# A two-block transformer kernel: ring order carried through, output squares summed one stage earlier, the start of each product stage rearranged

## The reference, cut to what matters

```python
def pre(t, mm, i, gi):            # adaptive norm ahead of a projection
    return rms_norm(t, g[gi]) * (1 + mm[:, :, i + 1]) + mm[:, :, i]
def post(t, y, mm, i, gi, wres):  # norm of the projection's output, then the residual
    return t + wres * mm[:, :, i + 2] * rms_norm(y, g[gi])
# first block, DEPTH = 2 layers
h  = post(h,  swiglu(pre(h,  m,  0, 0), ffn_wi[0], ffn_wo[0]), m,  0, 1, 0.5)
hc = post(hc, swiglu(pre(hc, mc, 0, 0), ffn_wi[0], ffn_wo[0]), mc, 0, 1, 0.5)
...   # attention mixers between w_in and w_o, on h (and hc unless last)
h  = post(h, o @ w_o, m, 3, 3, 1.0)
h  = post(h, swiglu(pre(h, m, 6, 4), ffn_wi[1], ffn_wo[1]), m, 6, 5, 0.5)
...   # the same for hc, unless last

# second block, DEPTH = 2 layers: SSD + mLSTM mixer, then gated linear attention
for i in range(DEPTH):
    h = _rmsnorm(x, norm_g[i, 0])
    h = mixer(h)          # ends in concatenate([y, hm], -1) @ w_out, or o @ w_out
    x = x + _rmsnorm(h, norm_g[i, 1])
    f = _conv_ffn(_rmsnorm(x, norm_g[i, 2]), ...)   # gelu(gate) * val after a 3-tap conv
    x = x + _rmsnorm(f, norm_g[i, 3])
# rms_norm(x, g) = x * rsqrt(mean(x * x) + eps) * g; the output is x
```

## Time and profile before

| | |
|---|---|
| median of 3 timed runs | 2901.91 us |
| the profiled execution | 2906.06 us |
| its span, first to last instruction | 2904.3 us |
| TensorE busy with matmuls | 2690.8 us, 93% |
| VectorE, ScalarE busy | 1311.2 us (45%), 1174.9 us (40%) |
| DMA moved | 375.50 MB, mean 129 GB/s |
| mean granted TensorE clock | 0.954 |

### The profile page before, as it was taken

How to read it: one execution, slowest core, us unless ns; L and a number is a source line. 1 busy time by engine, 2 the same in 40 slices (tenths; PEclk the granted TensorE clock), 3 DMA queues, 4 the chain that set the end, 5 groups by cost and what they waited for, 6 DMA issues and landing times. The chain is left out here.

```text
span 2904.3 us, 39475 instructions
## 1 busy us (share of the span) xinstructions
PE 2690.8 (93%) x16552; PEld 2294.4 (79%) x16552; DVE 1311.2 (45%) x1671; ACT 1174.9 (40%) x1622; POOL 42.4 (1%) x80
## 2 busy tenths in 40 slices
PE   5999998998999998999998989989977899898998
PEld 3677786876677785888786879979966899897998
DVE  3222235455322234322336654455555576555675
ACT  3222225444322225332235544444355465353653
POOL 2000000000000002000000000000000000000000
PEclk8999999999999998999999989989987999898999
DMA  8666422212566524232231225435400354341443
GB/s 277 212 208 217 152 73 87 59 59 80 174 206 204 170 102 99 82 103 87 87 102 59 88 92 191 179 124 183 149 1 30 125 191 166 116 146 59 156 166 114
DMA packets 277162, 375.50 MB, mean 129 GB/s; under 512 B 11020, under 2 KB 232696, under 8 KB 276896
## 3 DMA queue, kind: packets, MB, share of 16 engines
q1 hardware_dynamic: 228240, 300.50, 31.1%
q10 hardware_dynamic: 46576, 69.26, 7.1%
q0 software_dynamic: 2208, 3.73, 0.9%
HBM read 372.33 MB, written 1.16 MB: 129 GB/s over the span
## 5 line engine op out<-in xcount | busy, mean ns | idle before, releaser
L464 PE MATMUL ps<-uh,wh 128*128 128x256 f32 (+1 forms) x4160 | 1396.8, 336 | 54.2 <-DVE ul L834 30.8
L465 PE MATMUL ps<-ul,wh 128*128 128x256 f32 (+1 forms) x4160 | 1381.2, 332 | 0.0
L466 PE MATMUL ps<-uh,wl 128*128 128x256 f32 (+1 forms) x4160 | 1379.3, 332 | 0.0
L464 PEld LDWEIGHTS ps<-uh,wh 128*128 128x128 f32 x4160 | 800.2, 192 | 170.5 <-issue 70.0
L455 DVE TENSOR_TENSOR wl<-ring,wh 128x2048 fp32r<-128x2048 f32 x212 | 482.1, 2275 | 889.2 <-ACT wh L450 784.3
L466 PEld LDWEIGHTS ps<-uh,wl 128*128 128x128 f32 x4160 | 800.4, 192 | 73.2
L465 PEld LDWEIGHTS ps<-ul,wh 128*128 128x128 f32 x4160 | 800.7, 192 | 69.7 <-issue 0.7
L450 ACT ACTIVATE wh<-ring 128x2048 fp32r<-128x2048 f32 x156 | 298.4, 1914 | 714.3 <-PE ps L466 349.8
L1066 DVE TENSOR_TENSOR wl<-ring,wh 128x2048 fp32r<-128x2048 f32 x66 | 151.3, 2293 | 324.0 <-ACT uh L1084 286.1
L1063 ACT ACTIVATE wh<-ring 128x2048 fp32r<-128x2048 f32 x66 | 126.3, 1914 | 340.1 <-PE ps L466 320.7
L1493 ACT ACTIVATE wh<-ring 128x2048 fp32r<-128x2048 f32 (+2 forms) x38 | 70.0, 1842 | 122.4 <-PE ps L466 122.2
(11 more groups left out here) (315 smaller groups left out, 2033.6 us busy)
## 6 DMA issues: line engine op xcount, KB each, us to landing
ring<-in_ffn_wi_dram SPq DMA_DIRECT2D x88, 1024.0 KB, 7.5
arena<-in_w_ada_dram ACTq DMA_DIRECT2D x42, 1536.0 KB, 6.7
ring<-in_ffn_w_up_dram SPq DMA_DIRECT2D x44, 1024.0 KB, 7.2
ring<-in_ffn_wo_dram SPq DMA_DIRECT2D x20, 2048.0 KB, 7.8
ring<-in_ab_w_in_dram SPq DMA_DIRECT2D x13, 2048.0 KB, 7.8
ring<-in_ffn_w_down_dram SPq DMA_DIRECT2D x10, 2048.0 KB, 7.8
ring<-in_c_w_in_dram SPq DMA_DIRECT2D x6, 2048.0 KB, 8.0
ring<-in_w_in_dram SPq DMA_DIRECT2D x20, 512.0 KB, 6.0
```

What stands on the lines that cost most here:

```text
L464: pe.matmul(to, sh, mh, start=start and n == 0, stop=False)
L465: pe.matmul(to, sh, ml, start=False, stop=False)
L466: mm = pe.matmul(to, sl, mh, start=False, stop=stop and last)
```

## The change

Seven edits, all of them of order and place; the arithmetic of the result is the same but for the order of one sum and of the accumulation in `ab_out`.

1. **Ring order.** `first` is no more given by hand. Each matrix begins in the slot after the last tile of the one before, so its tile 0 goes into the slot that is freed first, and tile 1 into the other.
2. **Output squares.** `Residual.tensor` becomes `tail_tensor`, in the producing stage, after its last product: TensorE multiplies the sum of the first seven squares and then the last square by ones, both into one bank. VectorE adds one square fewer.
3. **`high_of(1)`** stands ahead of the squares of `h` where T = 256.
4. **Fill.** Chunks of the second granule stand between those of the first: chunk 0 after chunk 4 for T = 512; chunks 0, 1, 2 after chunks 2, 4, 6 for T = 256.
5. **Down.** For T = 256 the split of the down projection's first input goes into the unused half of `uh` and `ul`, with no wait for the up products, and the second granule's split of the down weights is moved behind the last gate.
6. **`ab_out`.** The SSD half of the inputs is made in VectorE's loop of the `mlstm` stage, and the products of granules 0 and 1 stand between the transposes.
7. **End.** The stage `residual` is merged into `finish`: transposes follow each update of `h`, ScalarE copies eight times 128 x 256, and four stores of 256 KB take the place of two of 512 KB.

```diff
         def planned(key, weights):
+            if order:
+                before = plan[order[-1]]
+                weights.first = (before.first + before.n) % RING
             plan[key] = weights
...
                     load(sp, w, (turn + 1) * RING + k, k)       # before
+                    load(sp, w, (turn + 1) * RING + k, w.slot(k))
...
                     self.post.scalar(act)
+                    if self.n_s == 1:
+                        high_of(1)
                     for k in range(KD):
 
                         act.wait_ge(h_updated.sem, h_updated.at(k + 1))
                         act.activation(self.sq[:, k, :], h[:, k, 0:T], ACT.Square).then_inc(h_squared.sem, 1)
-                        if k == 2:
+                        if k == 2 and self.n_s == 2:
                             high_of(1)
...
-                    if k == 0:
+                    if k in (0, KD - 1):
                         continue
                     dve.wait_ge(y_squared.sem, y_squared.at(k + 1))
...
-            def tensor(self, pe):
-                pe.matmul(self.sum_bank(), ones, self.acc, start=True, stop=True).then_inc(y_summed.sem, 1)
+            def tail_tensor(self, pe):
+                pe.wait_ge(y_added.sem, y_added.at(KD - 2))
+                pe.matmul(self.sum_bank(), ones, self.acc, start=True, stop=False)
+                pe.wait_ge(y_squared.sem, y_squared.at(KD))
+                pe.matmul(self.sum_bank(), ones, self.ysq[:, (KD - 1) % 2, :], start=False, stop=True).then_inc(y_summed.sem, 1)
...
+            return [] if norm.post is None else [4] if norm.n_s == 2 else [2, 4, 6]
...
                 for kk in range(KD):
                     norm.input_ready(pe, kk)
+                    last = chunk(0, kk)
+                    if kk in beside:
+                        chunk(1, beside.index(kk))
                 last.then_inc(prod.sem, 1)
+                for kk in range(len(beside), KD):
+                    last = chunk(1, kk)
+                last.then_inc(prod.sem, 1)
...
-                            if g == KF - 1:
-                                down.input_high(act, 0)
-                            down.high_ahead(act, g - (KF - 2))
+                        elif g == KF - 2:
+                            down.high_ahead(act, 0)
+                        else:
+                            down.input_high(act, 0)
...
+                    def scan_chunk(k):      # in the mlstm stage, once for each head
+                        dve.scalar_tensor_tensor(out=scan_made[:, k // 2, k % 2, :], in0=mixed[:, k, :], scalar=col("ssd_norm", k),
+                                                 in1=group_rstd[:, k // 4, :], op0=ALU.mult, op1=ALU.mult)
...
+                    turned(0)
+                    for q in range(half - 1):
+                        for i in range(2):
+                            pe.wait_ge(u_ready.sem, u_ready.at(2 * q + i + 1))
+                            for g in range(AHEAD):
+                                products(g, (KD * i + 2 * q, KD * i + 2 * q + 1), q == 0 and i == 0, False)
+                            if i == 0:
+                                turned(q + 1)
```

More of the change, by code:

```diff
@@ L315, in two_blocks, with __init__ @@
         class Weights:
-            def __init__(self, n, loads, parts=1, count=None, split=True, looped=True, first=0):
-                self.first = first
+            def __init__(self, n, loads, parts=1, count=None, split=True, looped=True):
+                self.first = 0
                 self.n, self.loads, self.parts, self.split = n, loads, parts, split
@@ L480, in tile_loaded @@
             if w.looped:
-                pe.wait_ge(ready[k].sem, ready[k].at((turn + 1) * 16 * w.parts))
+                pe.wait_ge(ready[w.slot(k)].sem, ready[w.slot(k)].at((turn + 1) * 16 * w.parts))
             else:
@@ L1222, in granule @@
                     ada.rows(pe, g)
-            first()
+            first_two()
             if ada is None:
-                turns(pe, KF, 4, granule, 1)
+                turns(pe, KF, 4, granule, 2)
             else:
-                for g in range(1, KF):
+                for g in range(2, KF):
                     granule(g // 4, g % 4)
@@ L1239, in ffn1 @@
             key = ("up", l, f)
-            down = Down(key, ("down", l, f), mid, T, tail, ada)
+            down = Down(key, ("down", l, f), mid, T, tail, dve_free, ada)
             pairs = 4 if ada is None else 2
@@ L1273, in granule @@
                         act.activation(gates[:, k, 0:T], ps[:, 2 * (k % pairs), 0:T], ACT.Silu).then_inc(gate_done.sem, 1)
+                        if not more and g == KF - 1:
+                            down.high_ahead(act, 1)
                     if ada is not None:
@@ L1294, in granule @@
                                           ALU.mult).then_inc(dve_free.sem, 1)
+                        if not more and g == KF - 1:
+                            down.low_ahead(dve, 1)
                     norm.vector(dve, lambda g: low_of(0, g))
@@ L1348, in tensor @@
                                         [((vh[:, kk, c], vl[:, kk, c]), (self.xh[:, kk, 0:self.T], self.xl[:, kk, 0:self.T]))
-                                         for kk in self.order], before=self.input_ready if g == 0 and m == 0 else None)
+                                         for kk in range(self.n_k)], before=self.input_ready if g == 0 and m == 0 else None)
                         if g == self.n - 1 and m < self.G - 1:
@@ L2050, in latent, with finish, _ @@
                 s_.passed(KD)
-        def finish():
-            tokens = Arena().take(ST, D)
+        def finish(r):
+            tokens = Arena(KD * T2).take(ST, D)
+            halves = [slice(0, D // 2), slice(D // 2, D)]
             with stage() as block:
+                @block.scalar
+                def _(act):
+                    if r is not None:
+                        r.scalar(act)
+                    for k in range(KD):
+                        act.wait_ge(pe_step.sem, pe_step.at(k + 1))
+                        act.activation(tokens[:, :, k * P:(k + 1) * P], ps[:, k, S:T2].rearrange("p (t c) -> p t c", t=ST),
+                                       ACT.Copy).then_inc(act_step.sem, 1)
@@ L2076, in _ @@
-                    sp.wait_ge(stored.sem, stored.at(16 * ST))
+                    for i, c in enumerate(halves):
+                        sp.wait_ge(act_step.sem, act_step.at((i + 1) * KD // 2))
+                        for t in range(ST):
+                            sp.dma_start(out[0, t * P:(t + 1) * P, c], tokens[:, t, c]).then_inc(stored.sem, 16)
+                    sp.wait_ge(stored.sem, stored.at(16 * 2 * ST))
         CF = Arena()
@@ L2085, in ffn2 @@
             key = ("up2", i)
-            down = Down(key, ("down2", i), mid2, S, tail)
+            down = Down(key, ("down2", i), mid2, S, tail, conv_done)
             n_ch = 2 * KF
@@ L2830, in ab_out @@
             AHEAD = 2
-            mem = Arena(ROWS_END + 2 * 2 * S + 12 * ML_HEADS + 2 * S)
-            made = mem.take(4, 2, S)
-            assert mem.at <= ARENA
+            made = Arena(HN_AT).take(2, 2, S)
             half = KD // 2
-            pairs = [p_ for q in range(half) for p_ in ((0, q), (1, q))]
             place_of = lambda i, q: slice(KD * i + 2 * q, KD * i + 2 * q + 2)
+            source = lambda i, q: made[:, q % 2] if i else scan_made[:, q]
             with stage() as block:
@@ L2858, in _, with turned @@
                 def _(pe):
-                    for q in range(half):
+                    def turned(q):
                         pe.wait_ge(act_step.sem, act_step.at(q + 1))
@@ L2864, in _, with products @@
                         tr.then_inc(pe_step.sem, 1)
-                    w.tensor(pe)
+                    def products(g, ks, start, stop):
+                        _, shaped = w.granule(g)
+                        vh, vl = shaped(wh[side(w.key, g)]), shaped(wl[side(w.key, g)])
+                        return multiply(pe, ps[:, g, 0:S], [((vh[:, kk, :], vl[:, kk, :]), (w.xh[:, kk, :], w.xl[:, kk, :])) for kk in ks],
+                                        start=start, stop=stop)
+                    turned(0)
@@ L2898, in ab_out @@
             w.done()
-        AB_ORDER = [k for q in range(KD // 2) for i in range(2) for k in (KD * i + 2 * q, KD * i + 2 * q + 1)]
         GM = Arena()
```

220 lines of the change are left out of this document (118 added, 102 removed).

## The result

The changed kernel takes 0.9853 times the time of the kernel before, with a 95% interval of 0.9828 to 0.9879. In microseconds its three runs are 2854.03, 2859.69 and 2864.61, against 2901.23 (median of four): 41.5 us less. (A fourth execution took 5613.93 us, nearly twice the others; no trace shows why, and it stands in no comparison.) In a later comparison the same kernel gave 2862.83 us and 0.9857 (0.9840 to 0.9873). The forecast was 2869 us, 2858 to 2883: 33 us of gain, about 42 measured (41.5 and 42.1 in the two comparisons).

What follows compares the result with a forecast made beforehand. TensorE, busy 2690.8 of 2904.3 us, was taken to bound the kernel, leaving 213.5 us idle to gain from. Terms of -14.3, -5, +1.9, -6.85, -5.5, -3.4 summed to -33.2 us: median 2901.9 to about 2869, range 2858 to 2883.

Steps and rivals of the forecast that it cites:

- edits 1 and 2, product to Ln: Ten boundaries, last product to Ln: falls to 3.1 us (T = 512) or 1.5 (T = 256); -14.3 us, ends -7 and -17.
- edit 3, Ln to product, T = 256: Five boundaries: splitting granule 1 before the squares of h saves between 2.75 and 12.5 us; -5 taken.
- edit 4, fill: First granules: -0.9 for T = 512, +2.8 at four T = 256 boundaries; sum +1.9 us, ends -2 and +5.
- edit 5, up to down: Waits of 1.45 us go at three places, 2.16 at two, a new one near 1 comes; -6.85 us, ends -2 and -9.
- edit 6, ab_out: Products begin near 2229.5 instead of 2240.72, granule 2 then waits for its split; -5.5 us, ends -1.5 and -7.
- edit 7, the end: Program end: barrier goes, most transposes and copies run beside the updates; -3.4 us, ends -1 and -4.
- the ring order gates nothing: Tile late in its new slot too, at the boundaries; first two edits worth 1 us, not 14.3; 2882 us, chance 0.07.
- the one that makes `ab_out` worth nothing: Clock stays at 0.51 through ab_out's 96 matmuls: no gain there, fills cost 5 us; 2877 us, chance 0.15.
- at the low clock only the 0.63 goes, -0.55: Sums of h, T = 256: TensorE is slower than ScalarE at the low clock, so each boundary gains just its idle time.
- up to 0.75 us late: T = 256 boundaries: five chunks of granule 1, 3.6 us, cover granule 2's split, so granule 2 starts late by this.
- The figure that I had named from the Trainium skill: Final stores: a transfer takes some 2.0 us plus bytes over 436 GB/s; half-size store saves another 0.6 us, left unsummed.
- the third rival: Shorter TensorE stops at boundaries put sums of h at clock 1.00: another -7.5 us, 2861 us, chance 0.12.

Runs made afterwards that it cites:

- the first experiment: Changed kernel with the ring order undone, each matrix's first slot again given by hand: 2877.57 us, 0.9915.
- the better version: Changed kernel without fill at T = 256, output squares summed in producing stage only there, ab_out's granule 1 held back, lead behind squares at two boundaries: 2847.79 us, 0.9808.

## Why the prediction was right, and where it was not

The time lay in the range, 6 to 10 us below the likeliest value. By its own terms, in us of the profiled span, first and second pair of profiles (changed against before):

| term | forecast | first pair | second pair | |
|---|---|---|---|---|
| edits 1 and 2, product to Ln | -14.3 | -13.8 | -13.0 | all of it edit 1 |
| edit 3, Ln to product, T = 256 | -5 | -7.2 | -5.5 | undoing it alone costs 0.6 to 2.2 |
| edit 4, fill | +1.9 | +3.4 (waits of 0.80 to 0.88) | +3.4 | T = 512 gave nothing |
| edit 5, up to down | -6.85 | -6.4 (8.67 to 2.27 of waits) | -6.4 | not by the waits named |
| edit 6, ab_out | -5.5 | -5.15 | -5.1 | not by interleaving |
| edit 7, the end | -3.4 | -3.4 (Ln to end 14.76 to 11.32) | -3.4 | not undone by itself |
| not in the sum | 0 | -13.8 | -10.2 | clock |

**The terms** of the first pair hold within 2.2 us each, and their sum, -32.6, is near the forecast's -33.2. That agreement is in part luck. With edit 3 at what undoing it alone costs, 0.6 to 2.2 us, the edits' own sum is 26 to 27.5 us, which is also what idle time and the added matmuls make (-27.2 and -26.6). The remaining 14 us or so of the 42 are clock, which the sum had at nothing: a forecast that had each term right would have said 2875 us, and the clock brought it to 2860. The rival that the ring order gates nothing fell with the first experiment, and the one that makes `ab_out` worth nothing fell by its size.

**Edit 2.** I gave it no figure of its own, but the working added -1.4 for three boundaries and +0.5 for one. With the 0.3 us that each other boundary with T = 512 pays, as its own figure of 3.1 against 2.9 implied, that is nothing: 31.82 and 31.93.

**Edit 3.** The step that failed is the price at the two clock levels: "at the low clock only the 0.63 goes, -0.55", "at the high clock up to 2.5". The runs show 1.2 at the low level and 0.1 to 0.5 at the high. Ahead of ffn1(1, 1) the sums start 0.3 us later after Ln than before, the idle 0.63 within them is gone, and their matmuls take 6.70 us in place of 7.57, since the clock rises before they end. So the edit's own worth is 0.6 to 2.2 us over the five, not 5; the rest of the -7.2 and -5.5 is clock, since 4.9 of it is there with the edit undone. Granted clock over them is 0.54 to 0.72 in the two profiles of the changed kernel, where before four of five boundaries had 0.50; here at that boundary (window, length, busy time, clock):

```profile
1695.43:1702.13 6.70, 6.70 (x16) 0.55 0.00 0
```

**Edit 4.** The one bound I named, "up to 0.75 us late", was met and passed by 0.1. The credit of 0.9 for T = 512 was wrong: the wait in question (0.98 us at in-projection 1) is before a chunk that the fill stands behind.

**Edit 5.** Size right, waits wrong, and so luck. I had the first wait, 1.45, gone at all three places and a new one of about 1 us at two. The first is gone at one place only and has shrunk to 1.14 at two; the second, 2.16, is gone at both, and no new one came. The two errors cancel.

**Edit 6.** Size right, mechanism wrong. I put the gain on products that begin at 1.2 instead of 12.6 us, and charged for the split of granule 2, which takes 4.24 us and has 1.4 to 2.9 of cover. The wait came (2.96). But the same stage with the transposes ahead of all products is 0.5 us shorter still, since its first product comes at 8.0 us in place of 12.6: VectorE no longer makes the SSD half in between, and the waits between the groups of transposes are 0.6 to 1.7 us. I left the SSD half's multiplications out of the working, and moving them was the whole of it: with the ring order alone, where they are not moved, the stage still takes 61.2 us. (No run moves them and nothing else.)

The row on the transposes speaks against the rival that I drew on the Trainium skill for ("TensorE: Matmul & The Clock Gate", Part 4, PE-mode transpose). With products between them the transposes ran at the high level (0.60 us for four, granted clock 1.00), without products at the low (1.11 to 1.12). That the transposes hold the clock down between products is not so here. Whether by themselves they count less as busy time, as the page has it, the runs do not show: without products there was also idle time of 0.6 to 1.7 us between the groups.

**Edit 7.** The last copy ends at 2854.70 and the span at 2857.9: 3.2 us, and 3.14 before. That is no comparison of 256 KB with 512 KB. SyncE issues the four stores in two pairs, each when four copies are done, so 512 KB are still to be moved after the last copy, as before. From issue to landing a store takes 2.6 us with 512 KB and 2.2 with 256 KB, each with another near it in the queue (KB each, median us). Before and after:

```profile
out_dram<-arena SPq DMA_DIRECT2D x2, 512.0 KB, 2.6
```

```profile
out_dram<-arena SPq DMA_DIRECT2D x4, 256.0 KB, 2.2
```

The figure that I had named from the Trainium skill ("DMA: Bandwidth & Descriptors", Anatomy of one DMA) stands there for transfers that GpSimd issues, and these are SyncE's; both stores here are faster than the 3.2 and 2.6 us that one would estimate by it. No run stores a smaller last piece, so what that would bring is open.

**The clock.** The rest is the direction of the third rival ("the clock rises sooner"), mostly at another place than I put it. Its price was 7.5 us at the sums of h, in edit 3. There the clock gave what edit 3 did not: 5.0 of the 7.2 us in the first pair and 4.9 of the 5.5 in the second. More lies in the stretch with the SSD and mLSTM stages (5.4 and 5.0 us) and in the other long stretches. What ties it to the edits is not settled. The ring order alone does not bring it: its profile, with TensorE busy for 2674.8 us against 2690.8 and 2689.6 in the two profiles of before, is of its fastest run, and the granted clocks of its six runs, 0.955 to 0.961, overlap those of before, 0.952 to 0.959. All runs of the changed kernel and its variants that were compared have 0.962 to 0.970, whichever single edit is undone or altered. Of the edits, 7 and the early making of the SSD half were never undone, and no run adds a single edit but the ring order to the kernel before. Two readings are left: fewer and shorter stops of TensorE of any kind, or an edit that was not tried.

## What to carry to other kernels

Divide every difference of spans into idle and busy time of the bounding engine before explaining it; here the waits account for about 27 of the 42 us and the granted clock for the rest. Before calling a smaller busy time clock, take out the instructions that were added or removed. Profile more than one execution: the one profile of the ring order alone was of its fastest run, 8.6 us below the median. Let the next matrix's first tile go into the slot that is freed first: one line took out four waits of 5 to 12 us. Work put between the steps of another piece is worth only what idle time it finds; if it shortens the stretch that covers the next split, it costs, as both the fill and `ab_out`'s interleaving did.

## What was not expected of the hardware

TensorE's busy time outside the ends of the boundaries (last product to Ln), where the matmuls are the same in all variants, was 2678.9 and 2678.6 us before, 2659.7 and 2665.1 in the changed kernel, and down to 2654.1 in the better version, with mean granted clocks of 0.954 to 0.970 over the spans. The two profiles of the unaltered changed kernel differ by 5.4 us in it, which is as much as most of the edits give. In `ab_out` a wait of 2.96 us, and with granule 1 held back one of 1.80 us, was followed by 3.41 us at a granted clock of 0.50, so that it cost more than itself. The waits of 1.45 and 2.16 us in ffn2(0) of the kernel before were not: the clock stayed at 1.00.
